# Where activations and weights begin within their SBUF partition, in a fused transformer block of rounded-float32 products

## The chip, the cores and the metric

One core of a Trainium2 chip runs one program. Its engines are TensorE (PE; its weight loads are listed apart as PEld), VectorE (DVE), ScalarE (ACT), GpSimd (POOL) and SyncE (SP, which here only issues DMAs). Activations and weights lie in SBUF, 128 partitions of bytes; an address below is always the byte within a partition, and all 128 partitions are laid out alike. The metric is the time of the whole program on the device in microseconds (us), lower is better.

## The reference

```
mod   = silu(c) @ W_ada + b_ada              # 6 x 2048 numbers: shift1, scale1, gate1, shift2, scale2, gate2
h     = RMSNorm(x) * (1 + scale1) + shift1   # x: 512 tokens x 2048
proj  = h @ W_in                             # 2048 x 7168: 8 retention heads (q, k, v, gate), 8 differential heads (q, k, v)
y_ret = silu(g) * GroupNorm(Retention(q, k, v))
y_dif = 0.8 * RMSNorm_head((softmax(q1 k1^T) - lambda softmax(q2 k2^T)) v)
x     = x + gate1 * (concat(y_ret, y_dif) @ W_out)      # 2048 x 2048
h2    = RMSNorm(x) * (1 + scale2) + shift2
x     = x + gate2 * (relu(h2 @ W1)^2 @ W2)              # 2048 x 8192 and 8192 x 2048
out   = RMSNorm(x)
```

All of it is float32.

## The kernel before

Activations are kept transposed: a tile is 128 features by 512 tokens, 2,048 bytes in a partition. Weights come from memory in chunks of 128 x 1024 (`raw`, four buffers), which are eight blocks of 128 x 128. One block takes 512 bytes of a partition.

A float32 product is made of three products of a shorter format, float32r, in which TensorE takes a column in one pass. ACT rounds each chunk to `w_hi` (line 898), DVE writes the rest `w_lo` = raw - w_hi (line 1226), both with two buffers of 4,096 bytes. Activations are split in the same way into `act_hi` and `act_lo` (16 tiles each), and in the MLP's second product into `u_hi` and `u_lo` (8 tiles each). `split_products` (lines 475 to 493) works through a chunk: for each of its eight blocks it multiplies by the high half (line 488) and by the low half (line 489), w_hi stationary both times; then eight products of w_lo with the high half (line 492). So a chunk is 24 matmuls of 512 moving columns, each with a weight load of its own, though lines 488 and 489 load the same block. Lines 579 to 612 and some of lines 488 to 492 do the same with 256 columns, where a tile is cut in two at the seams of stages. The first projection's chunks go through line 507, half of them whole in float32 through line 554 (`xy` moving, `raw` stationary). The heads' small products are lines 641 to 643 and 665 (scores), 682, 690 and 837 (transposes, with `ident_r` moving), 699 (probabilities, in float32) and 705 and 706 (the variance over a head: `sq_hi` and `sq_lo` moving, the constant `inv_hd` stationary).

The order of all work is written out by hand, one stream an engine, with semaphores between them; there is no scheduler. The matmuls run chunk after chunk; while one chunk is multiplied, ACT and DVE split the next.

Where a tensor lies follows from the order in which the function asks for it: each begins where the one before ended, rounded up to 32 bytes, and the first begins at byte 16,512, which is 128 past a multiple of 512. `in_turn` and the closed stacks let tensors take the same bytes at different times (act_lo and rows_out do, and u_hi takes those of the heads' tensors). The large tensors are all multiples of 512 bytes long. So before the change every one of raw, w_hi, w_lo, act_hi, act_lo, rows_out and xy begins 128 bytes past a multiple of 512. The small ones from vec to neg_lam take 3,072 bytes with their rounding, six times 512, so the tensors behind them, sq, hf, q_hi, q_lo, k_hi, k_lo, v_sb, u_hi and u_lo among them, begin 128 past as well. Only what lies among the small ones stands elsewhere: ones, inv_hd and ident_r begin 256 past.

Of the kernel before, what the change touches and what calls it, by code (L numbers as in the profile page):

```python
# [27 lines left out]
F32R = mybir.dt.float32r  # L28
# [5 lines left out]
P128 = 128  # L34
D = 2048
TOK = 512
KT = D // P128
# [22 lines left out]
BLOCKS = 8  # L60
# [90 lines left out]
N_VEC = 160  # L151
# [57 lines left out]
def block_kernel(nc, x_t, c, ada, weights, vecs, lams, rot, decay, ident_in, mask_in, out):  # L209
    with ExitStack() as ctx:  # L210
        def sb(name, shape, dt=F32):
            return ctx.enter_context(nc.sbuf_tensor(name, shape, dt))
# [2 lines left out]
            return ctx.enter_context(nc.semaphore(name))  # L215


        raw = sb("raw", [P128, NRAW, CHUNK])
        w_hi = sb("w_hi", [P128, NW, CHUNK], F32R)
        w_lo = sb("w_lo", [P128, NW, CHUNK], F32R)  # L220
        act_hi = sb("act_hi", [P128, KT, TOK], F32R)
        act_lo_at = ExitStack()
        act_lo = act_lo_at.enter_context(nc.sbuf_tensor("act_lo", [P128, KT, TOK], F32R))
        act_lo_at.close()
        rows_out = sb("rows_out", [P128, TB, D])
        xy = sb("xy", [P128, KT, TOK])
        vec = sb("vec", [P128, N_VEC])
        ones = sb("ones", [P128, P128])
        inv_hd = sb("inv_hd", [P128, P128], F32R)
        ident_r = sb("ident_r", [P128, P128], F32R)  # L230
        inv_d = sb("inv_d", [P128, 1])
        ident = ident_r[:].bitcast(F32)
        ln_shift = sb("ln_shift", [P128, 1])
        minus_half = sb("minus_half", [P128, TB])
        mod1 = sb("mod1", [P128, KT, 2])
        modr = sb("modr", [P128, 4, KT])
        amul = sb("amul", [P128, 2, KT])
        part1 = sb("part1", [P128, 20])
        partr = sb("partr", [P128, 8])
        tok_v = sb("tok_v", [P128, TB])  # L240
# [1 line left out]
        v_sum = sb("v_sum", [P128, TB])  # L242
        v_mean = sb("v_mean", [P128, TB])
        neg_lam = sb("neg_lam", [P128, 1])

        def in_turn(*groups):

            made = []
            for i, group in enumerate(groups):
                stack = ctx if i == len(groups) - 1 else ExitStack()  # L250
                made += [stack.enter_context(nc.sbuf_tensor(name, shape, dt)) for name, shape, dt in group]
                if stack is not ctx:
                    stack.close()
            return made
# [3 lines left out]
        sq, sq_head, ve = in_turn([("sq", pair, F32)], [("sq_head", row, F32), ("ve", row, F32)])  # L258
        hf, o_sb, sq_hi = in_turn([("hf", pair, F32)], [("o_sb", row, F32), ("sq_hi", row, F32R)])
        rot_a, rot_b = sb("rot_a", row), sb("rot_b", row)  # L260
        ssq, rs0 = in_turn([("ssq", row, F32)], [("rs0", row, F32)])
        r_all, rs1 = in_turn([("r_all", row, F32)], [("rs1", row, F32)])
        sq_lo = sb("sq_lo", row, F32R)
# [2 lines left out]
        rot_a, rot_b = rot_a[:], rot_b[:]  # L266
# [49 lines left out]
        scores_seen = sbh("scores_seen", [P128, 1])  # L316
        heads.close()

        u_hi = sb("u_hi", [P128, BLOCKS, TOK], F32R)
        u_lo = sb("u_lo", [P128, BLOCKS, TOK], F32R)  # L320
        relu = sb("relu", [P128, 2, TOK])
        usq = sb("usq", [P128, 2, TOK])
# [1646 lines left out]
```

## Time and profile before

| | |
|---|---|
| time, median of 3 runs | 2340.15 us (2340.06 to 2340.94) |
| the profiled execution's own time | 2340.64 us |
| its span, first to last instruction | 2338.8 us |
| PE busy | 2319.4 us (99%), 10432 matmuls |
| PEld busy | 1891.5 us (81%), 10432 loads |
| DVE busy | 1256.9 us (54%) |
| ACT busy | 721.6 us (31%) |
| mean granted TensorE clock | 0.999 of full speed |

A busy time of PE is not its useful time: a matmul's record goes on while the next one has begun, so the pace is read from the starts of successive matmuls, and not from their durations. A weight load is recorded with the line and tiles of the matmul that it serves.

### The profile page before, as it was taken

To read this page: it belongs to the slowest core of one execution; us is meant where nothing else is said; L and a number is where in the kernel's file an instruction comes from. 1 tells how busy PE (TensorE), PEld (TensorE's weight loads), DVE (VectorE), ACT (ScalarE), POOL (GpSimd) and SP (SyncE) were. 2 spreads that over 40 slices of the span, in tenths; PEclk is the share of its full clock that TensorE was granted. 3 is DMA by queue.
4 is the path that set the end of the run, shared out by engine and by line. 5 is a ranking of instruction groups with operands and counts; after the bars stand their busy time and mean duration, and the time that the engine had idled before them with its cause. 6 is when DMAs were issued, how large, how long until landed. Compare 5 with 4: busy or idle time off the path is not lost.

```text
span 2338.8 us, 28294 instructions
## 1 busy us (share of the span) xinstructions
PE 2319.4 (99%) x10432; PEld 1891.5 (81%) x10432; DVE 1256.9 (54%) x1578; ACT 721.6 (31%) x1013; POOL 90.5 (4%) x59
## 2 busy tenths in 40 slices
PE   8999999999999999999999999999999999999998
PEld 5588888887888888888888888888888888888887
DVE  8988888866667675633333333333333333333355
ACT  3333333344445322421321322222222222222233
POOL 0011112101010000000000000000000000000000
PEclk9999999999999999999999999999999999999999
DMA  9965767622223573222222232232222222322322
GB/s 389 409 241 211 253 250 261 230 82 81 81 81 107 199 286 119 99 99 94 95 99 99 90 99 99 92 99 96 99 99 90 99 99 93 98 96 99 99 90 99
DMA packets 89719, 327.21 MB, mean 140 GB/s; under 512 B 8641, under 2 KB 9153, under 8 KB 89665
## 3 DMA queue, kind: packets, MB, share of 16 engines
q1 hardware_dynamic: 89376, 326.34, 39.7%
q8 instruction: 35, 0.57, 0.1%
q10 hardware_dynamic: 290, 0.16, 0.0%
q14 instruction: 18, 0.15, 0.0%
HBM read 322.27 MB, written 4.19 MB: 140 GB/s over the span
## 4 chain that ended last, share of the span: by engine, by line
PE 94%; DMA 3%; DVE 1%; issue 1%; ACT 0%; POOL 0%; POOLq 0%; DVEq 0%; ACTq 0%
PE bank L488 30%; PE bank L492 29%; PE bank L489 29%; DMA prob<-ada 3%; PE bank L699 1%; PE bank L665 1%; PE bank L690 0%; PE bank L604 0%; PE bank L682 0%; PE bank L533 0%; PE bank L545 0%; DVE prob L1232 0%; PE bank L837 0%; DVE w_lo L1226 0%; PE bank L643 0%
## 5 line engine op out<-in xcount | busy, mean ns | idle before, releaser
L488 PE MATMUL bank<-act_hi,w_hi 128*128 128x512 f32 x2016 | 790.6, 392 | 0.0
L489 PE MATMUL bank<-act_lo,w_hi 128*128 128x512 f32 x2016 | 785.3, 390 | 0.0
L898 ACT ACTIVATE w_hi<-raw 128x1024 fp32r<-128x1024 f32 x393 | 415.0, 1056 | 834.0 <-PE bank L492 825.2
L1226 DVE TENSOR_TENSOR w_lo<-raw,w_hi 128x1024 fp32r<-128x1024 f32 x393 | 496.6, 1265 | 292.9 <-ACT w_hi L898 279.4
L492 PE MATMUL bank<-act_hi,w_lo 128*128 128x512 f32 x2016 | 498.2, 389 | 0.1
L488 PEld LDWEIGHTS bank<-act_hi,w_hi 128*128 128x128 f32 x2016 | 378.6, 188 | 80.6 <-ACT w_hi L898 1.5
L492 PEld LDWEIGHTS bank<-act_hi,w_lo 128*128 128x128 f32 x2016 | 378.3, 188 | 79.0 <-DVE w_lo L1226 0.5
L489 PEld LDWEIGHTS bank<-act_lo,w_hi 128*128 128x128 f32 x2016 | 378.6, 188 | 77.7
L488 PE MATMUL bank<-u_hi,w_hi 128*128 128x512 f32 (+1 forms) x1040 | 401.6, 387 | 0.0
L489 PE MATMUL bank<-u_lo,w_hi 128*128 128x512 f32 (+1 forms) x1040 | 400.2, 386 | 0.0
L1651 DVE SCALAR_TENSOR_TENSOR xy<-bank,modr,xy 128x512 f32 (+1 forms) x141 | 105.9, 751 | 412.1 <-PE bank L492 412.1
L492 PE MATMUL bank<-u_hi,w_lo 128*128 128x512 f32 (+1 forms) x1040 | 253.5, 386 | 0.0
L488 PEld LDWEIGHTS bank<-u_hi,w_hi 128*128 128x128 f32 x1040 | 195.4, 188 | 39.2
L489 PEld LDWEIGHTS bank<-u_lo,w_hi 128*128 128x128 f32 x1040 | 195.3, 188 | 39.1
L492 PEld LDWEIGHTS bank<-u_hi,w_lo 128*128 128x128 f32 x1040 | 193.3, 188 | 39.3
L1711 DVE TENSOR_TENSOR usq<-relu 128x512 f32<-128x512 f32 x64 | 44.3, 692 | 234.6 <-ACT relu L1155 234.6
L1232 DVE CUSTOM_DVE_ANT_0 ada_sb<-ada_sb,silu_c 128x2048 f32<-128x2048 f32 x64 | 154.0, 2420 | 0.8 <-DMA ada_sb<-ada 0.8
L1155 ACT ACTIVATE relu<-bank 128x512 f32<-128x512 f32 x64 | 38.2, 597 | 273.4 <-PE bank L492 273.4
L1817 POOL TENSOR_TENSOR tok_r<-tok_v,minus_half 128x2 f32<-128x2 f32 (+1 forms) x5 | 5.0, 1000 | 1570.8 <-DVE tok_v L1775 1400.7
L1431 DVE CUSTOM_DVE_ANT_0 bank<-bank,mask 128x512 f32<-128x512 f32 (+3 forms) x64 | 29.5, 523 | 49.2 <-issue 49.2
L1714 DVE TENSOR_TENSOR u_lo<-usq,u_hi 128x512 f32 (+1 forms) x64 | 44.3, 693 | 16.5 <-ACT u_hi L1157 16.2
L945 ACT ACTIVATE sq<-xy 128x512 f32<-128x512 f32 x29 | 18.3, 632 | 111.0 <-DVE xy L1651 111.0
(176 smaller groups left out, 1305.8 us busy)
## 6 DMA issues: line engine op xcount, KB each, us to landing
raw<-weights SPq DMA_DIRECT2D x400, 512.0 KB, 3.3
ada_sb<-ada SPq DMA_DIRECT2D x78, 1024.0 KB, 5.2
xy<-x_t SPq DMA_DIRECT2D x16, 512.0 KB, 4.7
prob<-ada SPq DMA_DIRECT2D x8, 1024.0 KB, 10.4
ada<-ada SPq DMA_DIRECT2D x7, 1024.0 KB, 8.2
out<-rows_out SPq DMA_DIRECT2D x7, 512.0 KB, 3.8
ada_sb<-ada SPq DMA_DIRECT2D x4, 512.0 KB, 11.5
decay_sb<-decay SPq DMA_DIRECT2D x8, 256.0 KB, 3.3
```

What stands on the lines that cost most here:

```text
L488: pe.matmul(acc, stationary, hi, start=first, stop=False)
L489: pe.matmul(acc, stationary, lo, start=False, stop=False)
L492: mm = pe.matmul(acc, w_lo[:, w, i * P128:(i + 1) * P128], hi, start=False, stop=last)
L665: mm = pe.matmul(acc[:, at:at + n], q[rows, queries], k[rows, 0:n], start=i == 0, stop=i == 2)
L898: nc.scalar.activation(w_hi[:, w], raw[:, r], ACT.Copy).then_inc(hi_ready, 1)
L1155: nc.scalar.activation(relu[:, t % 2], bank[t if spare is None else spare][:], ACT.Relu).then_inc(relu_ready, 1)
L1226: nc.vector.tensor_tensor(w_lo[:, w], raw[:, r], w_hi[:, w].bitcast(F32), ALU.subtract).then_inc(lo_ready, 1)
L1232: nc.vector.tensor_tensor_reduce(ada_at(r), ada_at(r), silu_c[:], 1.0, start, ALU.mult, ALU.add, to)\
L1431: op = nc.vector.tensor_tensor_reduce(acc[:, at:at + n], acc[:, at:at + n], mask[:, TOK - n:], 1.0, FLOOR, ALU.add, ALU.max, top[:, 4 * co ...
L1651: nc.vector.scalar_tensor_tensor(to, bank[t if spare is None else spare][:], gate_col, to, ALU.mult, ALU.add)\
L1711: nc.vector.tensor_tensor(usq[:, t % 2], relu[:, t % 2], relu[:, t % 2], ALU.mult).then_inc(usq_ready, 1)
L1714: nc.vector.tensor_tensor(u_lo[:, i], usq[:, t % 2], u_hi[:, i].bitcast(F32), ALU.subtract).then_inc(u_ready, 1)
```

## The change

No instruction is added, removed or moved, and none gets another shape; the order on each engine stays as it was. Addresses change, and one small tensor is put elsewhere:

- vec, mod1 and amul (896 bytes) are asked for first, so that raw, w_hi and w_lo begin at multiples of 512.
- A gap of 256 bytes puts act_hi at 256 past a multiple of 512, one of 320 bytes puts act_lo at 64 past. rows_out, xy, inv_hd and ident_r follow at 64 past.
- A gap of 320 bytes behind the small tensors puts sq, hf, rot_a, ssq, the heads' tensors (q_hi, q_lo, k_hi, k_lo, v_sb, v_tok, strips, prob) at multiples of 512.
- u_hi becomes a view 16 bytes into a tensor that begins at a multiple of 512. The 16 bytes behind it and a gap of 160 put u_lo at 192 past; relu and usq follow at 192.
- ones, a constant of 512 bytes that is read at the start alone, lies in rot_a, which is first written by the rotation of the first head.

```diff
+        vec = sb("vec", [P128, N_VEC])
+        mod1 = sb("mod1", [P128, KT, 2])
+        amul = sb("amul", [P128, 2, KT])
         raw = sb("raw", [P128, NRAW, CHUNK])
         w_hi = sb("w_hi", [P128, NW, CHUNK], F32R)
         w_lo = sb("w_lo", [P128, NW, CHUNK], F32R)
+        sb("ahead_of_hi", [P128, 64])
         act_hi = sb("act_hi", [P128, KT, TOK], F32R)
+        sb("ahead_of_lo", [P128, 80])
         act_lo_at = ExitStack()
         act_lo = act_lo_at.enter_context(nc.sbuf_tensor("act_lo", [P128, KT, TOK], F32R))
...
-        vec = sb("vec", [P128, N_VEC])
-        ones = sb("ones", [P128, P128])
...
-        mod1 = sb("mod1", [P128, KT, 2])
...
-        amul = sb("amul", [P128, 2, KT])
...
         neg_lam = sb("neg_lam", [P128, 1])
+        sb("fill", [P128, 80])
...
         rot_a, rot_b = sb("rot_a", row), sb("rot_b", row)
+        ones = rot_a[:, 0:P128]
...
-        u_hi = sb("u_hi", [P128, BLOCKS, TOK], F32R)
+        u_hi_at = sb("u_hi_at", [P128, 8 + BLOCKS * TOK], F32R)
+        u_hi = u_hi_at[:, 4:4 + BLOCKS * TOK].rearrange("p (a b) -> p a b", a=BLOCKS)
+        sb("ahead_of_u_lo", [P128, 40])
         u_lo = sb("u_lo", [P128, BLOCKS, TOK], F32R)
```

## Rows read from the trace of the kernel before

**Rows 1.** Chain that ended last, by engine and by line

```profile
PE 94%; DMA 3%; DVE 1%; issue 1%; ACT 0%; POOL 0%; POOLq 0%; DVEq 0%; ACTq 0%
```

**Rows 2.** Groups of PE, shapes apart: count | busy us, mean ns | idle before

```profile
L488 PE MATMUL bank<-act_hi,w_hi 128*128 128x512 f32 x2016 | 790.6, 392 | 0.0
L489 PE MATMUL bank<-act_lo,w_hi 128*128 128x512 f32 x2016 | 785.3, 390 | 0.0
L492 PE MATMUL bank<-act_hi,w_lo 128*128 128x512 f32 x2016 | 498.2, 389 | 0.1
L488 PE MATMUL bank<-u_hi,w_hi 128*128 128x512 f32 x1008 | 393.4, 390 | 0.0
L489 PE MATMUL bank<-u_lo,w_hi 128*128 128x512 f32 x1008 | 392.4, 389 | 0.0
L492 PE MATMUL bank<-u_hi,w_lo 128*128 128x512 f32 x1008 | 249.0, 389 | 0.0
L579 PE MATMUL bank<-act_hi,w_hi 128*128 128x256 f32 x32 | 8.0, 285 | 0.0
```

**Rows 3.** Windows, PE, DVE, ACT: us, busy (instructions), clock, DMA share, GB/s

```profile
500.00:600.00 100.00, 100.00 (x491) 80.20 (x490) 62.56 (x134) 45.82 (x95) 7.77 (x6) 1.00 0.24 79
1100.00:1200.00 100.00, 100.00 (x443) 82.81 (x442) 35.40 (x37) 29.16 (x35) 0.00 (x0) 1.00 0.29 98
2000.00:2200.00 200.00, 200.00 (x884) 165.59 (x883) 71.02 (x73) 49.52 (x56) 0.00 (x0) 1.00 0.29 97
```

**Rows 4.** Timeline of PE and PEld, 1,503 us: start us, us, instruction

```profile
1503.46 0.39 PE L488 MATMUL bank<-act_hi,w_hi 128*128 128x512 f32 x1
1503.46 0.19 PEld L489 LDWEIGHTS bank<-act_lo,w_hi 128*128 128x128 f32 x1
1507.08 1.98 PE L492 MATMUL bank<-act_hi,w_lo 128*128 128x512 f32 x8
1508.90 0.39 PE L488 MATMUL bank<-act_hi,w_hi 128*128 128x512 f32 x1
```

**Rows 5.** Timeline of PE at 111 to 117 us, the float32 products

```profile
111.58 5.74 PE L554 MATMUL bank<-xy,raw 128*128 128x512 f32 x13
...
114.59 2.31 PE L554 MATMUL bank<-xy,raw 128*128 128x512 f32 x5
```

**Rows 6.** Timeline of PE around 915 us, products of 256 columns

```profile
914.83 0.28 PE L579 MATMUL bank<-act_hi,w_hi 128*128 128x256 f32 x1
...
917.71 0.28 PE L579 MATMUL bank<-act_hi,w_hi 128*128 128x256 f32 x1
```

**Rows 7.** Timeline of PE at 360 us: head variance, and the chunk behind it

```profile
360.68 0.40 PE L705 MATMUL bank<-sq_hi,inv_hd 128*128 128x512 f32 x1
360.92 0.40 PE L706 MATMUL bank<-sq_lo,inv_hd 128*128 128x512 f32 x1
361.16 0.40 PE L488 MATMUL bank<-act_hi,w_hi 128*128 128x512 f32 x1
...
363.47 0.39 PE L488 MATMUL bank<-act_hi,w_hi 128*128 128x512 f32 x1
```

**Rows 8.** Longest waits: who for whom, us, times, longest

```profile
ACT w_hi L898 <- PE bank L492: 825.2, 239, 4.4
DVE w_lo L1226 <- ACT w_hi L898: 279.4, 158, 4.9
```

**Rows 9.** Chain of the first 130 us, its longest pieces: start, us

```profile
91.75 10.39 DMA prob<-ada
104.55 10.39 DMA prob<-ada
130.57 2.24 DVE w_lo L1226
```

## The prediction, made before the result was known

> **What bounds the kernel now.** I read the shares of the chain of waits first, then the groups of PE by shape, then windows over the late stages, and only then single starts in the timeline. The chain is 94% PE and 3% DMA [rows 1]. The DMA part lies in the first 130 us, where the adaLN rows arrive [rows 9]; nothing of it depends on where a tile lies within 512 bytes, and I leave these 130 us as they are. Behind them PE never stands idle: its window is full from 500 to 600 us as from 1,100 to 2,200, at the full clock, while DVE is busy 63% and then 35%, ACT 46% and 25 to 29%, and DMA a quarter to 29% of the time [rows 3]. ACT and DVE wait for PE, not PE for them [rows 8]. So the time is the number of matmuls times their pace, and only the pace can change it.
>
> The pace has a loss in it that busy time hides. In the MLP 24 matmuls of 512 columns, one chunk, start within 1,508.90 - 1,503.46 = 5.44 us [rows 4], 226.7 ns each; 884 in 200 us [rows 3] say the same. At 2.4 GHz 512 columns are 213.3 ns, so 13.3 ns of each are not streaming. Three more rows tell what kind of loss this is.
> - It does not grow with the length. 24 matmuls of 256 columns take 917.71 - 914.83 = 2.88 us, 120.0 ns each [rows 6], against 106.7 of streaming: 13.3 again. It goes with the matmul, or with its weight load, which is 128 columns in both.
> - It is not there in plain float32. Seven records of line 554, each two passes of 512 columns (426.7 ns), take 114.59 - 111.58 = 3.01 us [rows 5], 430 ns each: 3.3 over, though each has a load beside it too. So a load beside a matmul doesn't cost 13.3 ns as such. I guess that the two-pass product leaves the reading of its moving tile some slack, which the one-pass product doesn't have; the trace doesn't show that.
> - It is not a constant of the format. Around line 705, where the weights are inv_hd (128 bytes further on, modulo 512, than everything else), two matmuls take 361.16 - 360.68 = 0.48 us, 240 ns each, and the ten of the ordinary kind that follow take 363.47 - 361.16 = 2.31 us, 231 ns each, before 226.7 returns [rows 7]. All of these are float32r, 512 columns, with loads of 128 columns.
>
> The load of the next block starts with the matmul it runs beside (both at 1,503.46) and its record lasts 0.19 us [rows 4]. So two streams read SBUF together: 2,048 bytes of moving tile, and 512 of weights. Before, both begin at the same remainder modulo 512, always. My reading is that they meet in the same part of the memory for some of the load, that this costs 13.3 ns, and that where they begin and how they stand in time decides how often they meet.
>
> The Trainium skill says otherwise: SBUF — State Buffer, "Who interferes with whom", gives TensorE two independent read ports, one for the moving operand and one for weights, and says that PE and ACT never wait on anyone. By it the sum would be nothing, and the loss a fixed cost of the format. The trace agrees in so far as DVE and ACT, busy 63% and 46% in one window and 35% and 29% in another, don't show in the steady pace; but rows 7 show the pace of one form vary from 226.7 to 240 ns, which a fixed cost doesn't.
>
> **The change part by part.** No instruction is added, removed or moved; the terms are changes of pace.
> 1. The general products: 3 x 2016 with act tiles and 3 x 1008 with u tiles, 9,072 of 512 columns [rows 2], and nine groups of 32 with 256 columns like the one shown [rows 2], 288. Together 9,360. The whole loss is 9,360 x 13.3 ns = 124.5 us, 5.3% of the span.
>  The trace has no product with such offsets, so both ends come from nearest rows. At best the loss falls to the 3.3 ns of line 554 [rows 5]: 10.0 ns x 9,360 = 93.6 us gained. At worst all run like lines 705 and 706, 240 ns [rows 7]: 13.3 x 9,360 = 124.5 us lost. Between them I take that half of the loss goes, 6.7 ns each, 220 ns: 62.4 us gained. The reason: act_hi stands at 256 from the weights, as far as it can within 512, the others at 64, 16 and 192, so each separates the two beginnings, but the moving tile runs through all 512 bytes four times while the load goes through its 512 once; they must pass each other whatever their beginnings. That some meetings remain is why I don't take 216.6.
> 2. The heads' products (q, k at remainder 0, as the weights are; v_sb and prob with ident_r at 64): relative places hardly differ from before for q and k, and the float32 ones show no loss. inv_hd moves from 128 to 64 past its moving tile; 32 matmuls at up to 13 ns are 0.4 us. Taken at nothing.
> 3. DVE, ACT and DMA now write and read at 16, 64, 192 and 256. All of them have room: at 220 ns a chunk takes 24 x 0.220 = 5.28 us, in which DVE has about 2 us of work (35% of 5.44), ACT 1.6, and the chunk's DMA needs 29% of 5.44, 1.6 us [rows 3]. If all three grew by a tenth PE would still not wait. In the heads DVE has 63%, 3.4 of 5.44 us, which fits in 5.28 as well. What becomes late next is nothing: PE remains the bound.
> 4. vec, mod1 and amul in another place, ones in rot_a: nothing is waited for that wasn't. Taken at nothing.
>
> Sum: the profiled execution took 2340.64 us (span 2338.8 and 1.8 around it); less 62.4 is 2278.2. It stood 0.5 us above the median of the runs, within their own spread, so I forecast **2278 us**.
>
> **The rivals.**
> *The loss is fixed, or settles back.* If the 13.3 ns belong to the format, as the skill's rule has it, or if the streams fall again into the relation in time that gives 226.7 (rows 7 show that they return to it after a disturbance), nothing moves: 2340 us. For it: the steady pace is the same to a tenth of a nanosecond for act and u tiles, with 16 different tiles and eight blocks. Against it: those are all alike modulo 512, so they can't show an effect of it, and rows 7 vary. That the layout doesn't do what it says belongs here; the sums of the sizes (17,408 for raw, 50,432 for act_hi) say that it does.
>
> *The alternation costs more: slower.* Lines 488 and 489 alternate between the high and the low half, which stood at the same remainder and now stand 192 and 176 bytes apart. The steady 226.7 is reached only after about ten matmuls of one kind [rows 7]; if each change of offset throws the streams out of it, the 16 matmuls of a chunk run as in that transient, and the eight of line 492 may settle to something else again. All at 231 ns would be +4.3 x 9,360 = 40 us, 2381 us; all at 240 gives 2465. It decides as soon as the mean over the three kinds of a chunk is above 226.7. For it: 226.7 is the lowest steady pace in the trace, and every departure from it that rows 7 show is upward. Against it: the departures there begin with the one load that isn't aligned like the rest, and one offset (128) doesn't tell of 256, 64, 16 and 192.
>
> **How the numbers follow.** Forecast (some of the loss goes, from a few us to 93.6): 0.47. Fixed or settled again: 0.23. Slower: 0.30. The likeliest case's own range is 2247 to 2333. For 8 in 10 I take 2247, the bound from line 554, and go over no change up to 2385, just beyond the transient's pace: 0.46 + 0.23 + half of the slower case, 0.14. What is left out are paces between 231 and 240. A difference of 0.2%, 4.7 us, is about what a measurement of this kernel tells from none; the few us on either side that fall within it are in the numbers as rounded: faster 0.47, same 0.23, slower 0.30.
>
> **What would show it.** In the changed trace, take 24 starts in the MLP as in rows 4: 5.28 us is my forecast, 5.44 the first rival, 5.54 or more the second. Then apart: the alternation of 488 and 489 (pairs of high and low) against the run of 492, and the up product (act at 256 and 64) against the down product (u at 16 and 192); each may have its own pace, and I expect all of them below 226.7. Line 554 should stay at 430 ns and the first 130 us as they were; if the time changes there, the argument that only the pace counts was wrong. The forecast is wrong as well if the pace falls and PE begins to wait for hi_ready or lo_ready, which would show as idle time before lines 488 and 492 that is not there now [rows 2].

## The result, and the profile after

The changed kernel takes 2374.21 us (median of 4 runs, 2373.78 to 2374.75), the kernel before 2340.48 (4 runs, 2340.06 to 2340.94): the ratio is 1.0143, interval 1.0131 to 1.0155. It is slower by 33.7 us. The forecast was 2278, faster by 62.4 us; the time lies inside the stated range (2247 to 2385), but on the other side of no change.

The lines of the kernel's code have moved by six: 494, 495, 498, 560, 711 and 712 are now what 488, 489, 492, 554, 705 and 706 were. First the chain of waits of the changed kernel, by engine; in [rows 1] it reads 94% PE:

```profile
PE 95%; DMA 3%; DVE 1%; issue 1%; ACT 0%; POOL 0%; POOLq 0%; DVEq 0%; ACTq 0%
```

Nothing has taken PE's place. The groups of PE by shape, as in [rows 2] (count, busy us, mean ns, idle time before):

```profile
L494 PE MATMUL bank<-act_hi,w_hi 128*128 128x512 f32 x2016 | 800.5, 397 | 0.0
L495 PE MATMUL bank<-act_lo,w_hi 128*128 128x512 f32 x2016 | 791.4, 393 | 0.0
L498 PE MATMUL bank<-act_hi,w_lo 128*128 128x512 f32 x2016 | 506.8, 393 | 0.0
L494 PE MATMUL bank<-u_hi_at,w_hi 128*128 128x512 f32 x1008 | 396.4, 393 | 0.0
```

The counts are the same, there is still no idle time ahead of any of them, and each record is 3 to 5 ns longer. So the matmuls neither became more nor wait; they follow each other more slowly. The windows of [rows 3] show how much (PE, PEld, DVE, ACT, POOL busy with their instructions, clock, DMA share, GB/s):

```profile
500.00:600.00 100.00, 100.00 (x485) 79.42 (x484) 61.32 (x130) 45.46 (x95) 9.06 (x7) 1.00 0.23 78
1100.00:1200.00 100.00, 100.00 (x434) 81.08 (x433) 34.01 (x35) 27.06 (x32) 0.00 (x0) 1.00 0.28 95
2000.00:2200.00 200.00, 200.00 (x866) 162.43 (x865) 69.13 (x72) 48.56 (x55) 0.00 (x0) 1.00 0.28 94
```

PE is full in each, at the full clock, and gets 485, 434 and 866 matmuls done where [rows 3] had 491, 443 and 884, 1.2 to 2.0% fewer. DVE, ACT and DMA are a little less busy than before, since PE feeds them more slowly. The starts of a chunk tell the pace itself, as [rows 4] did (start us, us, instruction). The up product, with the act tiles at 256 and 64, then the down product, with the u tiles at 16 and 192:

```profile
1006.67 0.39 PE L494 MATMUL bank<-act_hi,w_hi 128*128 128x512 f32 x1
...
1010.37 2.01 PE L498 MATMUL bank<-act_hi,w_lo 128*128 128x512 f32 x8
1012.23 0.39 PE L494 MATMUL bank<-act_hi,w_hi 128*128 128x512 f32 x1
```

```profile
1400.46 0.39 PE L494 MATMUL bank<-u_hi_at,w_hi 128*128 128x512 f32 x1
...
1404.14 2.02 PE L498 MATMUL bank<-u_hi_at,w_lo 128*128 128x512 f32 x8
1406.00 0.39 PE L494 MATMUL bank<-u_hi_at,w_hi 128*128 128x512 f32 x1
```

24 matmuls take 5.56 us (231.7 ns each) with act tiles and 5.54 us (230.8) with u tiles, where [rows 4] had 5.44 (226.7). Of the 16 that alternate and the 8 behind them, no part is fast: with u tiles 3.68 us (230.0 ns) and 1.86 us (232.5).

To see the whole of it I took, over the starts of lines 494, 495 and 498 with 512 columns (488, 489 and 492 before), what the step to the next matmul is above 226.67 ns, and summed. Steps over 250 ns are left out: they stand where PE waited or a longer product follows, and add up to about 8 us in both kernels.

```
us above 226.67 ns, summed   act tiles   u tiles
before                          2.68       0.58
after                          28.46      11.62
```

The difference is 25.8 + 11.0 = 36.8 us, of which 33.7 arrive at the end. Most of what comes off is in the first 130 us, some 2.3 us (below).

### The profile page after: what moved, and what is told of

It reads as the page before. It is cut to its first block, busy times and chain, and to the rows that moved or that the text cites. A ratio compares the mean times of both kernels' runs of the same rounds, so it can differ in the third digit from the quotient of the medians.

```text
span 2372.5 us, 28300 instructions
## 1 busy us (share of the span) xinstructions
PE 2353.9 (99%) x10432; PEld 1892.0 (80%) x10432; DVE 1256.0 (53%) x1578; ACT 722.2 (30%) x1013; POOL 90.7 (4%) x59
## 4 chain that ended last, share of the span: by engine, by line
PE 95%; DMA 3%; DVE 1%; issue 1%; ACT 0%; POOL 0%; POOLq 0%; DVEq 0%; ACTq 0%
PE bank L494 30%; PE bank L498 30%; PE bank L495 30%; DMA prob<-ada 3%; PE bank L705 1%; PE bank L671 1%; PE bank L696 0%; DVE prob L1238 0%; PE bank L610 0%; PE bank L688 0%; PE bank L539 0%; PE bank L551 0%; PE bank L843 0%; PE bank L513 0%; PE bank L649 0%
## 5 line engine op out<-in xcount | busy, mean ns | idle before, releaser
L494 PE MATMUL bank<-act_hi,w_hi 128*128 128x512 f32 x2016 | 800.5, 397 | 0.0
L498 PE MATMUL bank<-act_hi,w_lo 128*128 128x512 f32 x2016 | 506.8, 393 | 0.0
L494 PE MATMUL bank<-u_hi_at,w_hi 128*128 128x512 f32 (+1 forms) x1040 | 404.5, 390 | 0.0
L498 PE MATMUL bank<-u_hi_at,w_lo 128*128 128x512 f32 (+1 forms) x1040 | 258.4, 391 | 0.0
L494 PEld LDWEIGHTS bank<-u_hi_at,w_hi 128*128 128x128 f32 x1040 | 195.4, 188 | 42.5
L498 PEld LDWEIGHTS bank<-u_hi_at,w_lo 128*128 128x128 f32 x1040 | 193.4, 188 | 43.1
L1720 DVE TENSOR_TENSOR u_lo<-usq,u_hi_at 128x512 f32 (+1 forms) x64 | 44.3, 692 | 18.7 <-ACT u_hi_at L1163 18.3
```

Source lines behind the costliest of these rows:

```text
L494: pe.matmul(acc, stationary, hi, start=first, stop=False)
L498: mm = pe.matmul(acc, w_lo[:, w, i * P128:(i + 1) * P128], hi, start=False, stop=last)
L1720: nc.vector.tensor_tensor(u_lo[:, i], usq[:, t % 2], u_hi[:, i].bitcast(F32), ALU.subtract).then_inc(u_ready, 1)
```

## The experiments

Four kernels measure only the pace (scans 1 to 4): they compute none of the block, load a few tiles, run rows of matmuls of one kind into one bank, mostly 48 at a time, and write something of the right shape; of each row I read the starts of the last 24, once they have settled. The others are the whole kernel with tiles at other places. "Place" is the distance in bytes from the weights' beginning to the moving tile's, modulo 512. The diffs are shortened to what matters.

**Scan 1: the pace at 32 places, and at 72 pairs of places.**

```diff
+for n in range(32):                # tile n begins 16 * n bytes from the weights
+    for j in range(48):
+        pe.matmul(bank, w[j % 8], at[n])
+for a, b in PAIRS:                 # chunks as the kernel's: 16 alternating, 8 with a alone
+    chunks(at[a], at[b], 3)
```

> A kernel that measures pace alone: it computes none of the block. 32 moving tiles of 512 columns in float32r begin 0, 16, ..., 496 bytes past a multiple of 512, weight blocks at multiples of 512. First 48 matmuls in a row for each tile, one load each; then chunks as in split_products (16 matmuls alternating between a high and a low tile, eight with the high one), three for each of 72 pairs of places. Theory 1 (the streams settle by themselves unless the offset between them keeps changing): after ten matmuls every single tile is at 226.7 ns, whatever its place, and so are pairs of equal places; pairs of different places are at 229 to 232 ns. Theory 2 (each offset has its own price, alternation doesn't matter): single tiles differ, and a pair is the mean of its two singles. Theory 3 (the start must be a multiple of 64 bytes, the rest is free): 0, 64, 128, ... at 226.7, all others above. Each of them allows a place below 226.7, which would be a faster kernel; the settled paces I expect, if there are others, are steps of 6.7 ns (220.0, 233.3).

Part of PE's timeline (start us, us, 48 matmuls; the tile's name is its place in bytes):

```profile
70.61 11.16 PE L76 MATMUL bank<-at64b,w 128*128 128x512 f32 x48
81.61 11.25 PE L76 MATMUL bank<-at80b,w 128*128 128x512 f32 x48
...
159.79 11.35 PE L76 MATMUL bank<-at192b,w 128*128 128x512 f32 x48
170.98 11.42 PE L76 MATMUL bank<-at208b,w 128*128 128x512 f32 x48
...
204.32 11.08 PE L76 MATMUL bank<-at256b,w 128*128 128x512 f32 x48
215.24 5.03 PE L76 MATMUL bank<-at272b,w 128*128 128x512 f32 x21
```

From row to row: place 64 takes 11.00 us for 48 (229.2 ns), place 192 takes 11.19 (233.1), place 256 takes 10.92 (227.5), its few slow ones at the start included. Settled, in ns:

```
place   0      16     32     48     64     80     96     112
      226.67 231.67 233.33 233.33 228.88 231.12 233.33 231.12
place 128    144    160    176    192    208    224    240
      232.29 233.33 234.25 233.33 233.33 234.62 233.33 226.67
place 256 and on: 226.67, and from there each value above once more
```

So the pace depends on where the tile begins, with a period of 256 bytes, not 512 (that it is the distance from the weights, scan 2 shows). act_hi's 256 is the same place as 0. Of the 72 pairs (64 of places from 0 to 112, and eight more) none went below 226.67: (256, 0) and (256, 256) stay there, (256, 64), which is the change's pair of act tiles, has 231.67, and (16, 192), its pair of u tiles, 230.54. The kernel's trace shows 231.7 and 230.8: the scan has the whole effect in it. Of the three theories none holds whole. Equal pairs don't all come back to 226.67, as the first has it, though pairs of different places do lie above, at 228 to 234 (but for 0 with 256). Single tiles do differ, as the second has it, but a pair is not the mean of its two singles. 64 has a loss, against the third.

**All activations at 256; the act tiles alone; the u tiles alone.** Each against the changed kernel (the gap behind the small tensors is changed with them, so that the tensors behind it keep their places):

```diff
 # all at 256
-        sb("ahead_of_lo", [P128, 80])
+        sb("ahead_of_u_hi", [P128, 64])
+        u_hi = sb("u_hi", [P128, BLOCKS, TOK], F32R)     # in place of u_hi_at, no ahead_of_u_lo
 # act tiles alone: u_hi and u_lo plain, at 0
+        u_hi = sb("u_hi", [P128, BLOCKS, TOK], F32R)
 # u tiles alone: act_hi and act_lo at 0
-        sb("ahead_of_hi", [P128, 64])
-        sb("ahead_of_lo", [P128, 80])
```

> act_hi, act_lo, u_hi and u_lo all begin 256 past a multiple of 512, weights at multiples. Theory 1 (alternating offsets keep the streams from settling): one offset for all, so 226.7 ns again and 2340 us, as before. Theory 2 (every offset from the weights has its own price): not 2340; line 498's products with act_hi at 256 took 231.7 ns on average in the changed kernel, by which all of it is about 2385 us. Theory 3 (multiples of 64 are free): 2340 us.

> act_hi at 256 and act_lo at 64 as in the changed kernel, u_hi and u_lo at multiples of 512 like the weights. Summed over starts in the two traces, the products with act tiles take 26 us more in the changed kernel and those with u tiles 11 us more, with some 3 us saved elsewhere. If the two pairs act apart, this one takes 2363 us. Theory 1 and theory 2 both say so; theory 3 (multiples of 64 are free) says 2340.

> u_hi at 16 and u_lo at 192 as in the changed kernel, act_hi and act_lo at multiples of 512 like the weights. If the pairs act apart, 2340 + 11 = 2351 us, with the MLP's first products back at 226.7 ns and the second at 229 to 235. Theory 3 (multiples of 64 are free, 16 isn't) says the loss is here: 2374 less what 16 bytes don't explain.

Measured: all at 256, 2336.64 us (2336.2 to 2337.17), ratio to before 0.9984 [0.9974, 0.9993]. Act tiles alone 2363.61 (2362.94 to 2363.79), 1.0099 [1.0082, 1.0115]. U tiles alone 2347.94 (2347.43 to 2348.55), 1.0032 [1.0019, 1.0044]. All at 256 has the pace of before, in the MLP (PE's timeline):

```profile
1499.91 0.39 PE L492 MATMUL bank<-act_hi,w_hi 128*128 128x512 f32 x1
...
1503.54 1.98 PE L496 MATMUL bank<-act_hi,w_lo 128*128 128x512 f32 x8
1505.35 0.39 PE L492 MATMUL bank<-act_hi,w_hi 128*128 128x512 f32 x1
```

24 in 5.44 us. Moving the activations by the greatest distance within 512 does nothing to the pace, neither good nor bad; my reason for expecting a gain from just that distance falls. The 3.8 us that this kernel is faster than before come from elsewhere (below).

**Scan 2: every 4 bytes, and other shapes and types.**

```diff
+for at in range(0, 256, 4): run("r", 128, 512, at, 0)       # float32r, place at
+for m in (96, 64, 32): ...                                  # fewer weight columns to load
+for n in (384, 256): ...                                    # fewer columns moving
+run(..., at, 128) for at in (0, 128, 192)                   # weights moved, too
+"f" float32, "b" bfloat16, "s" always the same weights: at 0, 32, 192
```

> A kernel that measures pace alone and computes none of the block; all in runs of 48 matmuls. First float32r with the moving tile 0, 4, ..., 252 bytes past a multiple of 512. The first scan had a period of 256 bytes, 226.7 ns at 0 and 240 and 228.9 to 234.6 between; if the unit is 16 bytes, the three steps inside each behave like the one they start in, or near it; a place below 226.7 would be a faster kernel. Then 96, 64 and 32 stationary columns in place of 128: if moving tile and weight load disturb each other, the 13.3 ns over streaming at place 0 shrink with the columns, to about 10, 7 and 3, and the differences between 0, 32 and 192 shrink as well; if it is a fixed cost of the format they stay at 13.3. 384 and 256 moving columns at 0: 173.3 and 120.0 ns. Weights at 128: the moving tile at 128 then takes the part that 0 had (226.7), if only the distance counts, and 0 and 192 take 232.3 and 228.9, the values of -128 and 64. Two-pass float32 (12 matmuls each): 429 ns at every place. bfloat16 (the format rate is the same, half the bytes): below 220 ns, every place alike, if the bytes read are what meets. The same block loaded 48 times: as with eight blocks in turn.

Of the 64 places of 4 bytes seven have 226.67 ns (0, 28, 60, 156, 236, 240, 252), the others 228.3 to 240.0; none is lower. With the weights at 128, a tile at 0, 128 and 192 has 232.1, 226.67 and 228.88; with the weights at 0, the places 128, 0 and 64 have 232.29, 226.67 and 228.88 in scan 1, so it is the distance that counts. Place 128 alone has a second value: in this scan, with the weights at 0, it is 233.33. With fewer weight columns the loss does not shrink: at 96 columns 230.0, 233.3, 228.3 (places 0, 32, 192), at 64 230.0, 230.8, 232.8, at 32 231.7, 233.3, 231.1. With 384 columns moving both places have 173.33; with 256 place 0 has 120.0, place 192 113.33, the faster. Always the same weights: 226.67, 233.33, 233.33, as with others. The two other types, in PE's timeline (start us, us, instruction and count):

```profile
887.35 31.07 PE L73 MATMUL bank<-x,raw 128*128 128x512 f32 x72
918.25 31.24 PE L73 MATMUL bank<-mov_b,w_b 128*128 128x512 bf16 x144
949.15 44.59 PE L73 MATMUL bank<-mov,w 128*128 128x512 f32 x192
```

72 records of two-pass float32 take 30.90 us, 429 ns each, the same at its three places (settled 429.1, [rows 5] 430); 144 of bfloat16 take 30.90 us, settled 215.8 ns each, at all three places. The dependence belongs to the one-pass float32r product. The Trainium skill gives a back-to-back gap of N over 2.4 GHz and some 2.5 ns (TensorE: Matmul & The Clock Gate, "Wait — 56ns, not 53.3ns?"), by which I estimate 215.8 ns for 512 columns. The bfloat16 rows, 215.8, agree with it; float32r, 226.7 at best, does not follow it.

**All at 0; all at 64; all at 192.** The pairs of high and low then have one place, and nothing alternates.

```diff
 # all at 0: no ahead_of_hi, no ahead_of_lo, u_hi and u_lo plain
 # all at 64 (192): one filler in front of act_hi and one in front of u_hi
-        sb("ahead_of_hi", [P128, 64])
-        sb("ahead_of_lo", [P128, 80])
+        sb("ahead_of_hi", [P128, 16])       # 48 for 192
+        sb("ahead_of_u_hi", [P128, 16])     # 48 for 192
```

> All of act_hi, act_lo, u_hi, u_lo, inv_hd and ident_r at multiples of 512, like the weights: the arrangement of before, moved as a whole by 128 bytes, but with inv_hd and ident_r now in line as well. By the scan's period of 256 it is the same as e_same256: 2337 us. If the place itself counted and not the distance, it would be neither 2337 nor 2340.

> Activations at 64, one place for all. Theory 1, that a constant offset settles: 2337 us. Theory 2, that each offset has its own price, as the first scan shows (228.9 ns at 64): 9,072 x 2.2 ns = 20 us more, 2357 us.

> Activations at 192, one place for all. Theory 1: 2337 us. Theory 2 with the scan's 233.3 ns: 9,072 x 6.7 ns = 60 us more, 2397 us, slower than the changed kernel though nothing alternates.

Measured: all at 0, 2336.75 us (2336.26 to 2337.65), 0.9983 [0.9974, 0.9993]; all at 64, 2355.51 (2355.02 to 2355.87), 1.0064 [1.0047, 1.0081]; all at 192, 2393.98 (2393.43 to 2394.4), 1.0228 [1.0211, 1.0245]. The MLP of the last one, in PE's timeline:

```profile
1500.43 0.39 PE L492 MATMUL bank<-act_hi,w_hi 128*128 128x512 f32 x1
...
1504.17 2.03 PE L496 MATMUL bank<-act_hi,w_lo 128*128 128x512 f32 x8
1506.03 0.39 PE L492 MATMUL bank<-act_hi,w_hi 128*128 128x512 f32 x1
```

24 in 5.60 us are 233.3 ns, the scan's value for 192; all at 64 runs at 228.9 (the mean of its steps from 1,000 to 2,200 us), its value for 64. 9,072 matmuls by 233.33 - 226.67 are 60.4 us; measured over all at 0: 57.2. No alternation is needed for a loss: the place alone can cost.

But the place alone does not explain the act tiles' part. act_hi stands at 256, which alone has 226.67 ns; only act_lo, a third of the products, stands at 64 with 228.9, which would be 2.2 x 2,016 = 4.5 us. The act tiles alone lose 26.9 us (next paragraph), so some 22 of them come with the alternation between the two places. The 8 of the w_lo run, all at 256, take 1.86 us in the changed kernel, 232.5 ns each, where all at 256 has 1.81; scan 4 will show that at place 0 it can take up to ten matmuls to settle. The u tiles are different: 16 and 192 alone have 231.67 and 233.33, and the pair's 230.5 is no more than they cost alone.

The two halves of the change add up: act tiles alone are 2363.61 - 2336.75 = 26.9 us over all at 0, u tiles alone 11.2, together 2336.75 + 38.1 = 2374.8; the changed kernel has 2374.2.

All at 0 also shows what the 128 of inv_hd had cost before. PE's timeline at the head variance, as [rows 7]:

```profile
357.85 0.39 PE L707 MATMUL bank<-sq_hi,inv_hd 128*128 128x512 f32 x1
358.08 0.39 PE L708 MATMUL bank<-sq_lo,inv_hd 128*128 128x512 f32 x1
358.30 0.39 PE L490 MATMUL bank<-act_hi,w_hi 128*128 128x512 f32 x1
...
360.57 0.39 PE L490 MATMUL bank<-act_hi,w_hi 128*128 128x512 f32 x1
```

Two in 0.45 us and the ten that follow in 2.27 (227 ns), where [rows 7] has 0.48 and 2.31. Over all 16 pairs and the ten behind each these starts are 1.2 us closer together than in the kernel before.

**Scan 3: which meeting could it be?** With 32 weight columns at every 16 bytes; other numbers of columns; and two tiles and two weights in turn, for what counts: the weights that a matmul uses, or those loaded beside it.

```diff
+(32, 512, (at,), (0,)) for at in range(0, 256, 16)
+(128, n, (0 or 192,), (0,)) for n in (496, 480, 464, 448, 320)
+(128, 512, (0, s), w) for s in (16, 64, 128, 192) for w in ((0, s), (s, 0), (0, 0))
```

> A kernel that measures pace alone and computes none of the block; runs of 48 float32r matmuls. Scan 2 refuted that the loss shrinks with the columns of the weight load (32 columns still 231 to 233 ns). First, 32 stationary columns with the moving tile at 0, 16, ..., 240. If the weight load takes part with its start alone, the paces are those of 128 columns at each place; if with its end (the last bytes it read), the table is shifted by 128 bytes (a load of 32 columns ends 384 bytes earlier); if the load takes no part and only successive moving tiles count, all 16 are equal. Second, 496, 480, 464, 448 and 320 moving columns at 0 and 192: if the settled pace only takes values in steps of 6.7 ns, then 496 columns (206.7 ns of streaming) are at 220.0 and 464 (193.3) at 206.7, and 480 and 448 between them are at the next step up. Third, moving tiles alternate between 0 and s (16, 64, 128, 192), with the weight blocks alternating as 0, s (each tile then stands at distance 0 to its own weights, and at s or -s to the load that runs beside it) or as s, 0 (distance 0 to the load beside it), or always at 0. If what meets is the moving tile and the load beside it, the order s, 0 is at 226.7 ns for every s and 0, s is not; if it is a tile and its own weights, the other way about.

With 32 columns the places run from 226.67 (80, 112, 176) to 240.0 (224), and 0 has 231.67: the place matters as much as with 128, but the order is another, and neither the old one nor the old one shifted. The columns moving give 223.33, 216.67, 208.92, 202.5 and 146.67 at 0, and 220.0, 215.75, 213.33, 202.2 and 146.67 at 192: no step of one size. Alternating at s = 192, tiles with their own weights' place equal have 231.67 and the load beside equal 233.33, at s = 64 both 231.67; the one 226.67 among the twelve is s = 192 with all weights at 0. Both expected patterns fail. What meets what inside the chip isn't settled by this.

**Scan 4: is the pace at a place always the same?** Before each row of 48, one to three float32 products of 100 to 217 columns shift the start in time, ten times for each of five places.

```diff
+for _ in range(d % 3 + 1): pe.matmul(bank1, raw, x[:, 0:100 + 13 * d])
+for j in range(48): pe.matmul(bank0, w[j % 8], mov[at])     # at 0, 28, 64, 192, 240
```

> A kernel that measures pace alone and computes none of the block. e_same240 ran at 233 and 237 ns a matmul and differently from run to run, though the scan had the place 240 at 226.7. Here float32r runs of 48 matmuls at the places 0, 240, 64, 192 and 28 each follow ten different disturbances (one to three float32 matmuls of 100 to 217 columns). If a place has several steady paces and the moment at which the run begins picks one, 240 shows more than one (226.7, 233.3, 236.7), and a single scan of it was luck; at 0, where every kernel so far came back to it, all ten end at 226.7. If instead the loop structure of the full kernel made the difference, 240 is at 226.7 ten times.

Places 0, 28, 64 and 192 came back to 226.67, 226.67, 228.9 and 233.33 ten times of ten; place 240 had 236.67 eight times and 233.33 twice, and in scan 1 226.67. A place can have several steady paces; which one it falls into depends on how it starts.

**All at 240, and all at 28, two places that the scans had at 226.67.**

```diff
-        act_hi = sb("act_hi", [P128, KT, TOK], F32R)
+        act_hi_at = sb("act_hi_at", [P128, 8 + KT * TOK], F32R)
+        act_hi = act_hi_at[:, 7:7 + KT * TOK].rearrange("p (a b) -> p a b", a=KT)   # 28 bytes
 # for 240: ahead_of_hi of 56, and [:, 4:...]; act_lo, u_hi and u_lo alike
```

> act_hi, act_lo, u_hi, u_lo at 240 past a multiple of 256, weights and the rest at 0. In the first scan the tiles at 240 reached 226.7 ns after one matmul, those at 256 after nine. In e_zero, matmuls that are not yet settled cost 2.4 us in all over 226.7 ns each. If the quick settling holds from any disturbance, this saves about 2 us: 2334.7 against 2336.7. If it was the chance of the state it started from: 2336.7. If the heads' float32 work disturbs more, since it stays at 0: up to 2339.

> act_hi, act_lo, u_hi and u_lo at 28 past a multiple of 256, weights, inv_hd and the heads' tensors at 0. In the last scan every run at 28 ended at 226.7 ns after ten different disturbances, as at 0, and was there after one to three matmuls where 0 took up to ten. If what a place does after many disturbances carries over to the full kernel (and 240 failed only because one scan of it was luck), this takes 2336.7 less most of the 2.4 us that unsettled matmuls cost in e_zero: 2335. If the table of the scans holds in the full kernel for multiples of 256 alone, it is above 2341, as e_same240 was (2359 to 2419).

Measured: all at 240, six runs from 2359.07 to 2419.63 us, median 2408.27, all at a granted clock of 0.999. The fastest of them is still 18.5 us over before. That the pace differs from run to run, as scan 4's did at 240, is the likely reason for the spread; only one of the six, of 2418.23 us, has a trace. Its PE timeline:

```profile
1501.10 0.40 PE L499 MATMUL bank<-act_hi_at,w_hi 128*128 128x512 f32 x1
...
1504.89 2.06 PE L503 MATMUL bank<-act_hi_at,w_lo 128*128 128x512 f32 x8
1506.78 0.40 PE L499 MATMUL bank<-act_hi_at,w_hi 128*128 128x512 f32 x1
```

24 in 5.68 us, 236.7 ns, the slowest pace seen in any of these kernels, though scan 1 had the place among the best. The guess that quick settling in a scan saves 2 us missed. All at 28: 2344.49 us (2343.42 to 2345.25), 1.0017 [1.0008, 1.0027]. In its trace:

```profile
1498.84 0.39 PE L498 MATMUL bank<-act_hi_at,w_hi 128*128 128x512 f32 x1
...
1502.48 2.00 PE L502 MATMUL bank<-act_hi_at,w_lo 128*128 128x512 f32 x8
1504.32 0.39 PE L498 MATMUL bank<-act_hi_at,w_hi 128*128 128x512 f32 x1
```

The 16 that alternate take 3.64 us (227.5 ns), the 8 of the w_lo run 1.84 (230.0). Here, too, the forecast 2335 missed: the scans' 226.67 at 28 doesn't carry over to the kernel. In the w_lo run the kernel reads successive tiles that lie one behind the other; the scan read one tile again and again. That may be the difference, but no run tries it by itself. Of the places tried in the kernel only 0 and 256 hold 226.7 in both parts.

**Before, with the large tiles at multiples of 512.** This is the kernel before with a filler of 384 bytes in front of raw. All tiles move together, so their distances from each other stay, but they now begin at multiples of 512. The changed kernel has raw and the weights at multiples of 512.

```diff
+        sb("ahead", [P128, 96])
         raw = sb("raw", [P128, NRAW, CHUNK])
```

> The kernel before, pushed on by 384 bytes as a whole: every large tensor at multiples of 512, inv_hd and ident_r 128 past as they were in relation to the rest. e_zero is 3.9 us faster than before; between their traces 2.2 us of that appear in the first 130 us, and 1.45 us around the head variance, where inv_hd is out of line. If the first part comes from transfers or engines that like multiples of 512 bytes, this kernel has that and not the other: 2338.3 us, first 130 us shorter by 2.2. If it comes from elsewhere in the new order of the tensors: 2340.5.

Measured: 2338.25 us (2337.55 to 2339.03), 0.999 [0.9981, 0.9999], 2.3 to 2.4 us less. Where from: the first product with w_lo, at which the w_lo of [rows 9] arrives, starts at 130.48; in the kernel before it is at 132.86. This experiment, then before:

```profile
130.48 2.12 PE L493 MATMUL bank<-act_hi,w_lo 128*128 128x512 f32 x8
```

```profile
132.86 1.88 PE L492 MATMUL bank<-act_hi,w_lo 128*128 128x512 f32 x7
```

And the window from 60 to 100 us, where DMA bounds (PE alone: us, busy, clock, DMA share, GB/s), of this experiment, of before and of after:

```profile
60.00:100.00 40.00, 40.00 (x127) 1.00 1.02 420
```

```profile
60.00:100.00 40.00, 39.99 (x125) 1.00 1.03 409
```

```profile
60.00:100.00 40.00, 40.00 (x127) 1.00 1.03 420
```

With destinations at multiples of 512 the queues move 420 GB/s, not 409, at nearly the same busy share. The engines are no faster for it: VectorE's instruction that reads prob takes 2,350 ns in the kernel before and 2,348 here. The issues of the page say the same (us from issue to landing at the end), here of after; the kernel before has 10.4 and 8.2 in these two lines, the pieces of [rows 9] 10.39:

```profile
prob<-ada SPq DMA_DIRECT2D x8, 1024.0 KB, 10.0
ada<-ada SPq DMA_DIRECT2D x7, 1024.0 KB, 7.8
```

## Why the prediction was wrong

**What bounds the kernel: right.** PE still is the bound, no idle time has come before lines 494 and 498, and the 33.7 us are a matter of pace alone but for the first 130 us. The upper bound of 240 ns is also the highest pace that the scans found; it was taken from a single row, so that it fits so well is partly luck.

**Step 1 failed: the general products' pace, and with it the sign of the sum.** The term was 62.4 us gained; by the traces it is 36.8 us lost. I took that "half of the loss goes", because "act_hi stands at 256 from the weights, as far as it can within 512". Scan 1 shows a period of 256: the greatest distance is 128, and 256 is none; all at 256 has the pace of before. And distance 0, from which the change moved the tiles away, is the lowest pace found, not the worst: of 64 places and 72 pairs none is below 226.67 ns for 512 columns. So nothing could be gained, and the act pair (256, 64) and the u pair (16, 192) had only losses to choose from: +5.0 and +3.9 ns by their scan values, 26.9 + 11.2 = 38.1 us by the kernels with one part each. The lower bound, the 3.3 ns of line 554, belongs to another type and was out of reach.

**The reading behind it: half right.** Right in that the distance between moving tile and weights changes the pace (scans 1 and 2 vary nothing else, row against row), and in that two-pass float32 is free of it: line 560 still has 429 ns. That the two reads meet in the same part of the memory no run shows. Wrong in two ways. If the two met for as long as a load lasts, fewer weight columns would lose less; with 32 columns 13 of 16 places are still 2.2 to 13.3 ns above 226.67. And I took 13.3 ns as the price of meeting always and looked for less from any other place; they turned out to be the least that 512 columns pay at any place I tried. One product does get below 13.3: 256 columns at 192, with 113.3, 6.7 over its 106.7 of streaming. The kernel has 288 of that shape, too few to matter. [Rows 7], the only direct evidence on another distance, pointed upward, and I used it for the upper bound and the slower rival alone; place 128 has 232.3 or 233.3 ns when settled.

**Step 2, the heads' products.** inv_hd's move I took at nothing, with 0.4 us as its whole price. Its real cost before was about 1.2 us, summed over the starts in the traces. All at 0 is 2336.75, and before with the large tiles at multiples of 512 is 2338.25; inv_hd's place is most of these 1.5 us, and the other 0.3 is within the spread of either. Not only its 32 matmuls run slower, but the ten behind each pair, too, as rows 7 had shown.

**Step 3, DVE, ACT and DMA: right** where I looked, behind the first 130 us. **The first 130 us: wrong.** "nothing of it depends on where a tile lies within 512 bytes": it does, by 2.3 us, now that the adaLN rows and the weights land at multiples of 512. The sum nearly closes with it: before 2340.5, less 2.3 for the transfers and 1.2 for inv_hd's place, is 2337.0 against 2336.75 for all at 0; 2336.75 plus 26.9 and 11.2 is 2374.8 against 2374.2.

**The rivals.** "The loss is fixed, or settles back" fell: paces settle, but at another value. "The alternation costs more: slower" had the sign and nearly the size: 231 ns and 2381 us, against 231.4 and 2374. Its mark, 24 starts in 5.54 us or more, is there. Its mechanism fits the act tiles: 256 and 64 alone have 226.7 and 228.9, together 231.67, and some 22 of their 26.9 us are of the alternation, not of either place. It isn't the whole cause: all at 64 and all at 192 alternate between nothing and lose 14.8 and 53.3 us, and the u tiles at 16 and 192 lose no more together than each place does alone. So that its 231 ns, a transient's, fits the u tiles too is luck. All this gave its 0.30 a better claim than I saw: with 226.7 the lowest pace in the trace and each departure upward, slower should have been likelier than faster.

The Trainium skill's rule of two independent ports (SBUF — State Buffer, "Who interferes with whom"), by which PE never waits, would have forecast no change. Float32r does not behave so: 226.7 to 240.0 ns for nothing but a distance. Bfloat16 and two-pass float32 agree with it, at the three places tried. What inside the chip makes the difference is open.

The best version is all at 256 or all at 0, 2336.7 us: 0.16% below before and 1.6% below the changed kernel. None of its gain is from a faster settled pace; it is the transfers' and inv_hd's.

## What to carry to other kernels

Before moving tiles to cure a loss in the pace, measure the pace at many places in a kernel of nothing else: one such run showed both that no place beat the one of before and what the change would cost. For float32r products of 512 columns with 128 weight columns, keep the operands at a distance of a multiple of 256 bytes from their weights, and small constants among them (inv_hd) as well; tiles that take turns need the same distance modulo 256; a place that only happens to be as fast in a scan (28, 240) needn't hold in the kernel. When every departure in a trace goes one way, take that as evidence on what another change of the same thing does.

## What the runs showed of the hardware

- A float32r product of 512 columns has a settled pace of 226.7 to 240.0 ns by the distance of its operands modulo 256 bytes, and at distance 0 needs 1 to 10 matmuls to get there after a disturbance (scan 4). Bfloat16 has 215.8 and two-pass float32 429 at the three places tried (0, 32, 192).
- Two tiles in turn at different distances can be slower than either alone: 0 and 64 have 226.67 and 228.88, in turn 231.67.
- A place may have more than one settled pace: 240 showed 226.67, 233.33 and 236.67, 128 showed 232.3 and 233.3, and a kernel that stands at 240 spreads over 60 us from run to run.
- With 256 columns moving, another place is the fast one (192: 113.3 ns, 0: 120.0), and with 32 weight columns 0 has 231.67 and 80 has 226.67, so no place is best for all shapes.
- Transfers into tiles at multiples of 512 bytes ran at 420 GB/s and landed in 10.0 us; into tiles 128 past them it was 409 GB/s and 10.4 us. No other place was tried.
